# Eight taps of a 31-tap convolution moved from VectorE to ScalarE and GpSimd in a one-core decoder step

## The reference, cut to what matters

```python
hn = rmsnorm(x, g_mix)
z = hn @ w_in                       # 1024 -> 5 x 1024: xa, u_glu (two parts), gate_a, gate_b
v = u_glu[..., :D_CONF] * jax.nn.sigmoid(u_glu[..., D_CONF:])
v_c, new_conf = causal_dwconv(v, conf_buf, w_conf_dw, b_conf_dw)    # 31 taps per channel
y_b = jax.nn.silu(layernorm(v_c, g_conf_ln, b_conf_ln)) @ w_conf_pw + b_conf_pw
m = jax.nn.sigmoid(gate_a) * y_a + jax.nn.sigmoid(gate_b) * y_b
h = x + m @ w_out
y = h + moe(rmsnorm(h, g_ffn), ...)          # top 4 of 32 experts
```

## Time and profile before

| | us |
|---|---|
| median of 3 runs (1339.78 to 1343.15) | 1340.11 |
| span of the profiled execution | 1338.6 |
| TensorE busy (matmuls) | 1295.3, 97% |
| VectorE busy | 508.0, 38% |
| ScalarE busy | 179.5, 13% |
| GpSimd busy | 79.1, 6% |

### The profile page before, as it was taken

One profiled execution on the slowest core, in us unless ns is written; L12 is line 12 of the kernel. 1 busy time (PEld: TensorE's weight loads), 2 busy tenths in 40 slices (PEclk: granted clock), 3 DMA queues, 4 the chain that ended last, 5 costly groups with the idle time before them and its releaser, 6 DMA issues.

```text
span 1338.6 us, 19293 instructions
## 1 busy us (share of the span) xinstructions
PE 1295.3 (97%) x7441; PEld 648.4 (48%) x7442; DVE 508.0 (38%) x981; ACT 179.5 (13%) x325; POOL 79.1 (6%) x107
## 2 busy tenths in 40 slices
PE   6999689999999999999999999999999999999996
PEld 4777467564544444444444444444444444443532
DVE  2899996542232232232323232222222232223232
ACT  3111126220100000101000000000000000010102
POOL 2532220120000000000000000000000000000000
PEclk9999889999999999999999999999999999999999
DMA  9934312468999999999898989898989898989671
GB/s 291 322 127 152 136 63 95 190 248 342 396 414 374 413 374 388 398 361 423 364 417 360 419 358 418 357 422 364 423 362 423 355 422 356 420 357 421 261 316 37
DMA packets 84376, 439.59 MB, mean 328 GB/s; under 512 B 7983, under 2 KB 30639, under 8 KB 35427
## 3 DMA queue, kind: packets, MB, share of 16 engines
q1 hardware_dynamic: 83219, 437.11, 81.4%
q0 software_dynamic: 976, 1.96, 0.5%
q10 hardware_dynamic: 144, 0.00, 0.0%
HBM read 437.46 MB, written 2.43 MB: 329 GB/s over the span
## 4 chain that ended last, share of the span: by engine, by line
PE 82%; DVE 8%; issue 6%; ACT 2%; DVEq 1%; DMA 0%; POOL 0%; SPq 0%; ACTq 0%; POOLq 0%
PE ps L1001 33%; PE ps L1060 16%; PE ps L979 11%; PE ps L1084 7%; PE ps L992 4%; DVE ws L1305 4%; PE ps L788 4%; PE ps L1053 3%; PE ps L910 2%; PE ps L805 1%; DVEq L1304 1%; DVE ws L1277 1%; PE ps L918 1%; PE ps L937 0%; DVE ws L1289 0%
## 5 line engine op out<-in xcount | busy, mean ns | idle before, releaser
L1001 PE MATMUL ps<-ring,ws 128*64 128x512 f32 x2032 | 451.5, 594 | 0.0
L1001 PEld LDWEIGHTS ps<-ring,ws 128*64 128x64 f32 x2032 | 141.5, 137 | 298.9 <-issue 298.9
L1060 PE MATMUL ps<-ring,ws 128*64 128x512 f32 x992 | 218.6, 592 | 0.0
L1476 DVE TENSOR_TENSOR acc<-ps,acc 128x1024 f32<-128x1024 f32 x48 | 58.8, 1224 | 285.9 <-PE ps L1084 285.9
L805 PE MATMUL ps<-ws,ring 128*128 128x288 f32 x640 | 159.7, 413 | 0.7 <-issue 0.7
L1456 DVE TENSOR_SCALAR ws<-ps 64x1024 f32<-64x1024 f32 x32 | 38.9, 1217 | 310.5 <-PE ps L1001 310.5
L979 PE MATMUL ps<-ws 128*128 128x64 bf16 x2304 | 145.3, 227 | 0.0
L979 PEld LDWEIGHTS ps<-ws 128*128 128x128 bf16 x2304 | 141.8, 170 | 2.9 <-issue 0.8
L805 PEld LDWEIGHTS ps<-ws,ring 128*128 128x128 f32 x640 | 123.8, 194 | 35.5 <-issue 0.8
L1060 PEld LDWEIGHTS ps<-ring,ws 128*64 128x64 f32 x992 | 71.3, 138 | 143.4 <-issue 143.2
L1305 DVE SCALAR_TENSOR_TENSOR ws<-ws,par x240 | 113.7, 549 | 0.0
(11 more groups left out here) (187 smaller groups left out, 611.2 us busy)
## 6 DMA issues: line engine op xcount, KB each, us to landing
ring<-in_w_gate SPq DMA_DIRECT2D x127, 1024.0 KB, 7.0
ring<-in_w_up SPq DMA_DIRECT2D x127, 1024.0 KB, 9.2
ring<-in_w_down SPq DMA_DIRECT2D x124, 1024.0 KB, 7.0
ring<-in_w_in SPq DMA_DIRECT2D x20, 1024.0 KB, 11.3
ring<-in_w_conf_pw SPq DMA_DIRECT2D x4, 1024.0 KB, 6.4
ring<-in_w_out SPq DMA_DIRECT2D x4, 1024.0 KB, 6.7
ws<-in_w_down SPq DMA_DIRECT2D x2, 1024.0 KB, 9.5
acc<-in_x_prompt SPq DMA_DIRECT2D x2, 512.0 KB, 4.2
```

Source lines behind the costliest of these rows:

```text
L1001: ins = nc.tensor.matmul(ps[m * CAP:(m + 1) * CAP, bk + h, :], x_e[:, b, 2 * q + t, :], w[:, m, t, h * 512:(h + 1) * 512], start=False, st ...
L1060: ins = nc.tensor.matmul(ps[h * CAP:(h + 1) * CAP, bk, :], hid_t[:, b, k, :], w[:, h * 512:(h + 1) * 512], start=False, stop=(k == NT - 1))
L1476: V.tensor_tensor(acc[:, i, :], ps[:, bk:bk + 2, :].rearrange("p h n -> p (h n)"), acc[:, i, :], ALU.add).then_inc(s_add, 1)
```

## The change

The prompt's taps are split: `KV` = 23 taps (0 to 22) stay with VectorE, eight (23 to 30) go elsewhere. For each tile ScalarE makes eight products of 256 columns, each a copy with a per-channel scale, into two groups of four "lanes". GpSimd folds them: group 0 += group 1 (1024 columns), the first two lanes += the last two (512), then lane 0 + lane 1 (256) into `part`. VectorE adds `part` to its own sum at the end of each pair of tiles.

The lanes use the memory of `gate_a`, `part` that of the first 2048 words after it, where `st_v`, the rows of new state, are put later. So there are new waits: ScalarE's products of a tile wait for the gated unit (`s_v`) and for the fold of the tile before (`s_fold`), its first gate waits for all folds, and its copies of the state rows wait for the whole convolution (`s_conv`, `N_CONV`). ScalarE makes the products of two tiles after the `vb` of the second. GpSimd folds after the gated units of a pair and before the tap products of that pair (for the first pair, after them).

```diff
+LANES = 4
+KV = KC - 2 * LANES
...
+        lanes = ga_w[:, 0:2 * LANES * T_P].rearrange("p (g l t) -> p g l t", g=2, l=LANES)
+        part = ga_w[:, TW:TW + NT * T_P].rearrange("p (c t) -> p c t", c=NT)
...
-        CONV_MID = 2 * (KC // 2) + 4
+        CONV_MID = 2 * (KV // 2) + 4
+        CONV_TILE = KV + 3
         N_STORES = 16 * 14
-        N_CONV, N_XC = NT * (KC + 2), 2 * NT * KA
+        N_CONV, N_XC = NT * CONV_TILE, 2 * NT * KA
...
+                def fold(c):
+
+                    for cc in (c, c + 1):
+                        pool.wait_ge(s_lane, 2 * cc + 2)
+                        pool.tensor_tensor(lanes[:, 0], lanes[:, 0], lanes[:, 1], ALU.add).then_inc(s_fold, 1)
+                        pool.wait_ge(s_fold, 3 * cc + 1)
+                        pool.tensor_tensor(lanes[:, 0, 0:2], lanes[:, 0, 0:2], lanes[:, 0, 2:4], ALU.add).then_inc(s_fold, 1)
+                        pool.wait_ge(s_fold, 3 * cc + 2)
+                        pool.tensor_tensor(part[:, cc, :], lanes[:, 0, 0, :], lanes[:, 0, 1, :], ALU.add).then_inc(s_fold, 1)
...
+                    if c:
+                        fold(c)
                     if c == 0:
                         pool.wait_ge(empt_v, EV("par"))
...
+                    if c == 0:
+                        fold(c)
...
+                    if c % 2:
+                        for cc in (c - 1, c):
+                            act.wait_ge(s_v, 2 * cc + 2)
+                            for g in range(2):
+                                if cc:
+                                    act.wait_ge(s_fold, 3 * cc - (2 if g else 0))
+                                for n in range(LANES):
+                                    j = KV + g * LANES + n
+                                    ins = act.activation(lanes[:, g, n, :], vx[:, cc, j:j + T_P], ACT.Copy,
+                                                         scale=par[:, cc, W_DW + j:W_DW + j + 1])
+                                ins.then_inc(s_lane, 1)
...
+                act.wait_ge(s_fold, 3 * NT)
                 for c in range(4):
                     act.activation(gate_a[:, c, :], empty(f"ga{c}")[:, 0:T], ACT.Sigmoid).then_inc(empt_a, 1)
 
+                act.wait_ge(s_conv, N_CONV)
                 for name, st, b, r in (("vp", st_v, 0, HC), ("vs", st_v, 1, T_S), ("xp", st_x, 0, HA),
...
-                    for j in range(KC):
+                    for j in range(KV):
                         past = 0
-                        if j == KC // 2:
+                        if j == KV // 2:
...
+                    dve.wait_ge(s_fold, c * 3 + 6)
+                    for n in range(2):
+                        dve.wait_ge(s_conv, base + (2 * KV + 3 + n))
+                        V.tensor_tensor(vc[:, c + n, 0:T_P], vc[:, c + n, 0:T_P], part[:, c + n, :], ALU.add).then_inc(s_conv, 1)
```

More of the change, by code:

```diff
@@ L246, in build @@
         s_conv = sem("conf_conv_steps")
+        s_lane = sem("tap_products_in_lanes")
+        s_fold = sem("lanes_folded")
         s_tap = sem("sample_tap_products_ready")
@@ L522, in _ @@
                     else:
-                        pool.wait_ge(s_conv, (c - 2) * (KC + 2) + CONV_MID)
+                        pool.wait_ge(s_conv, (c - 2) * CONV_TILE + CONV_MID)
                     for cc in (c, c + 1):
@@ L553, in _ @@
                     if c == 1 or c % 2 == 0:
-                        pool.wait_ge(s_conv, (c // 2 + 1) * 2 * (KC + 2))
+                        pool.wait_ge(s_conv, (c // 2 + 1) * 2 * CONV_TILE)
                     if c > 1:
@@ L1281, in _ @@
                     dve.wait_ge(s_v, c * 2 + 4)
-                    base = c * (KC + 2)
-                    for j in range(KC):
+                    base = c * CONV_TILE
+                    for j in range(KV):
                         past = 0
-                        if j == KC // 2:
+                        if j == KV // 2:
                             dve.wait_ge(s_tap, c + 2)
@@ L1295, in _ @@
                             past = 4
-                        elif j > KC // 2:
+                        elif j > KV // 2:
                             past = 4
@@ L1303, in _ @@
                             else:
-                                dve.wait_ge(s_conv, base + (2 * (j - 1) + n + 1 + (past if j != KC // 2 else 0)))
+                                dve.wait_ge(s_conv, base + (2 * (j - 1) + n + 1 + (past if j != KV // 2 else 0)))
                                 V.scalar_tensor_tensor(y, x, w, y, ALU.mult, ALU.add).then_inc(s_conv, 1)
+                    dve.wait_ge(s_fold, c * 3 + 6)
+                    for n in range(2):
+                        dve.wait_ge(s_conv, base + (2 * KV + 3 + n))
+                        V.tensor_tensor(vc[:, c + n, 0:T_P], vc[:, c + n, 0:T_P], part[:, c + n, :], ALU.add).then_inc(s_conv, 1)
                 dve.wait_ge(empt_a, EA("xa1"))
```

## The result

| | before | after |
|---|---|---|
| median, us | 1340.38 (4 runs) | 1360.37 (4 runs, 1357.69 to 1361.74) |
| ratio, 95% interval | | 1.0143 [1.0127, 1.0158] |
| span of the profiled execution | 1338.6 | 1358.5 |
| loop of the 31-tap convolution on VectorE | 40.37 to 168.29, 127.9 long | 41.92 to 170.78, 128.9 long |
| subtraction of the mean starts | 173.72 | 193.24 |

The account below looks back on a forecast made before the run. VectorE's convolution was taken to bound the kernel before the mean; folds repay the saved taps and the added wait puts five TensorE jobs behind it: 1338.6 + 19.9 + 1.5 = 1360.0 us, range 1351 to 1368.

Parts of the forecast that it names:

- VectorE alone: 31-tap convolution on VectorE: 64 steps removed save 25.5 us, eight additions cost 3.2, so 22.3 us shorter.
- What the folds take: GpSimd's fold additions beside VectorE's convolution: 14336 columns at 1.87 ns take 26.9 us of VectorE's time, bounds 24.2 and 31.1.
- What leaves the loop: GpSimd's channel-tile sums (L557) move behind the convolution, giving VectorE back 2.7 us.
- Loop: VectorE's 31-tap convolution: 129.8 us long, ending at 170.2 instead of 168.3 (167.5 and 174.4 with the bounds).
- Other engines: GpSimd needs 26 us a pair against VectorE's 32.4 and keeps ahead; TensorE's ga0 may stand 1 to 5 us, covered.
- The added wait: ScalarE's state-row copies wait for the convolution; five TensorE jobs start at 170.8, the mean ends at 193.6: +19.9 us.
- The rest moves along: After the mean's subtraction: gate blocks, w_out and its successors, expert loads included, move by the same 19.9 us.
- The rule of the prediction: Whole kernel: time follows the convolution's end; the change needs an end before 150.3 to gain.
- folds that cost little: Rival: long GpSimd additions let VectorE's steps through, convolution ends at 143.3, time 1333.1, gain 7 us; 7 in 100.
- the cases between: Folds take 7 to 20 us of VectorE's time, kernel time 1340 to 1353; 8 in 100.
- GpSimd as the bound: Rival: at 10 us a fold GpSimd needs 36 us a pair, VectorE waits, time 1372; 10 in 100.
- the hidden wait: Rival: TensorE's five jobs don't stand behind the bank of vp0, the mean waits for GpSimd alone, 1351.1; 3 in 100.

Follow-up runs that it names:

- without folds: The changed kernel with each GpSimd fold addition cut to one column per lane, products and waits kept, folded taps left out of the result: 1333.4 us, ratio 0.9929.
- the same additions beside 31 taps: The kernel before, all taps on VectorE, plus three GpSimd additions per tile (1024, 512, 256 columns) on data nobody else uses: 1371.5 us, ratio 1.0213.
- The wait alone: The kernel before plus one line, ScalarE's state-row copies waiting for the whole convolution: 1357.6 us, ratio 1.0108.
- short folds: The changed kernel with the same sums, every fold addition cut into pieces of 256 columns, seven a tile instead of three: 1356.7 us, ratio 1.0120.
- four taps: The changed kernel with four taps per tile moved instead of eight, folded sums in memory of their own, without the added wait: 1343.7 us, ratio 1.0021.
- eight and ten taps on TensorE: The kernel before with eight or ten taps per tile of the last pair multiplied on ScalarE, summed on TensorE: 1333.9 and 1330.8 us.
- neither folds nor wait: The changed kernel with one-column folds (folded taps left out) and sums in memory of their own, so without the added wait: 1321.3 us, ratio 0.9855.
- sums in memory of their own: The changed kernel, complete, with part in the gate-block weights' memory, loaded after the convolution, so state-row copies don't wait for it: 1345.2 us, ratio 1.0021.
- twelve taps: The kernel before with twelve taps per tile of the last pair multiplied on ScalarE and summed on TensorE: 1334.6 us, ratio 0.9951.

## Why the prediction was right

It said 1360.0 and the time was 1360.4. By its steps:

- **VectorE alone** (64 steps fewer, eight additions more: 22.3 us saved). Before, less the sums' 3.2 us, is 124.7; without folds it is 101.6. That is 23.2 saved. With GpSimd quiet the additions took 0.75 for two.
- **What the folds take** (26.9, within 24.2 and 31.1). 128.9 - 101.6 = 27.3 us, 1.90 ns a column. The row of L557, nearest in operands, gave 1.87 and was close; the same additions beside 31 taps cost 2.02, so the agreement to 0.4 us is better than the method. The Trainium skill has an exclusive lock on the shared port pair, held for a whole instruction (SBUF — State Buffer, section "Who interferes with whom"). The trace agrees in kind: unrelated additions on GpSimd lengthened the loop by 29.0 us, and two steps lost 2.17 us beside a 1024-column addition of 2.44. It doesn't agree with the price that the prediction drew from the rule, whole durations (31.1): part of the standing is GpSimd's, as the additions of 3.38 and 3.94 us show. The prediction's sign for the 1024-column fold, 2.1 to 2.5 us, held for five of the eight; the others took 2.53, 2.72 and 3.38.
- **What leaves the loop** (2.7). The wait alone measured 3.2.
- **Loop** (129.8, to 170.2). 128.9, to 170.8. The forecast was 0.9 too long; but the loop began 1.5 later than before, because TensorE's first 32 w_in instructions took 10.98 us and not 9.76 (and began 0.3 later). In the other runs they took 9.47 to 11.05, whatever the edit, so I take it for no effect of the change. In each microsecond from 21 to 24 us three of these instructions are under way, and not five or six as before, while the granted clock reads 1.00 in both profiles; the cause stays open.
- **Other engines** (GpSimd 26 us a pair, margin 6; `ga0` stands 1 to 5 us). GpSimd's last taps waited 8.4 us for VectorE, and `ga0` stood 4.7. Both as said. A second short stand, 3.2 us before the state rows (they need columns that GpSimd packs until 143.35), I had not named; it was covered too.
- **The added wait** (five jobs at 170.8, 22.1 us long with the clock, then the mean). They started at 171.6 and took 21.1, so the subtraction was at 193.24 for 193.6 forecast. The clock, as the earlier trace rows before and here after:

```profile
155.00:171.00 16.00, 0.00 (x0) 0.00 (x0) 16.00 (x39) 0.10 (x1) 0.00 (x0) 0.50 0.00 0
171.00:173.00 2.00, 1.43 (x3) 1.17 (x4) 2.00 (x9) 2.00 (x5) 0.54 (x1) 0.50 0.00 0
...
175.00:177.00 2.00, 2.00 (x10) 1.56 (x9) 0.28 (x2) 0.00 (x0) 2.00 (x5) 1.00 0.16 27
```

  After 22.8 us idle TensorE was at 1.2 GHz (0.50) when work came, at 0.63 on average from 173 to 175 and at 2.4 GHz (1.00) from 175. The five jobs lost 1.5 us by it (21.07 for 19.57); the forecast had 2.5, with the mean's part.
- **The rest moves along** (19.9). w_out started at 264.00, 19.4 after the 244.59 of before. It ran at the lower clock there, 4.94 us for 3.66, 1.3 more that was not in the forecast; of these 20.7 us some 0.8 were made up later, and the span grew by 19.9.

So the mechanism was right, and the agreement to 0.4 us is in part luck: the late start of the loop (1.5) and the clock at w_out (1.3) were not in the forecast, and the shorter loop (0.9), the cheaper clock (1.0) and the 0.8 at the end go the other way.

The split that the prediction gave only as a sum is now measured, each median against before beside it. Both in place: 20 us slower. With the wait and without folds it is 8 faster, so folds cost 28 us on top of the wait; with folds and without the wait 4 slower, so the wait costs 16 on top of the folds. Both away is 20 faster. Alone, wait and folds on the kernel before cost 16 and 30.

The rule of the prediction, "time = 1340.1 + (end of the convolution - 150.3)" held where the wait was present: 1332.7 for no folds (measured 1333.4), 1356.4 for the wait alone (1357.6), 1356.3 for short folds (1356.7). All three lie 0.4 to 1.2 us over the rule, and so does before beside them (1341.3 and 1341.4 for 1340.1).

The rivals: folds that cost little, and the cases between (7 to 20 us), fell by the 27.3 and 29.0 us; GpSimd as the bound by the 8.4 us that it waited; the hidden wait by the wait alone. Their shares (7, 10 and 3 in 100) can't be judged from one case.

## What to carry to other kernels

VectorE's multiply-adds and GpSimd's additions, both on SBUF, weren't parallel work here (1.9 to 2.0 ns of VectorE per GpSimd column): before moving one to the other, price the GpSimd columns at what a VectorE step loses beside them, from any overlap in the trace. Summing tree-wise on GpSimd took 1792 columns for eight products of 256, almost a column for each column moved, so it gave back all that it took. And when a new buffer borrows the memory of a later one, follow the wait through every in-order queue: here one line on ScalarE held five jobs of TensorE and cost as much as a real piece of work. TensorE had a hole of 15.8 us; given the sums of ten taps in the last pair, it took them without slowing VectorE, and the kernel was 0.7% faster (ratio 0.9929).

## What the runs showed of the hardware that was not expected

TensorE's clock at w_out. In every profile TensorE stands 2.4 to 2.8 us before it, for VectorE's last merge. In some profiled executions the 64 instructions then take 3.66 us (before, four taps, eight and ten taps on TensorE, neither folds nor wait), in the others 4.94 to 5.35. The length of the stand doesn't sort them: in the run with sums in memory of their own it was 2.36 with the fall, in that with neither folds nor wait 2.83 without. The windows of before and of after show the difference in the granted clock:

```profile
244.00:246.00 2.00, 1.41 (x28) 1.08 (x32) 0.38 (x1) 1.05 (x2) 0.24 (x1) 1.00 1.01 426
```

```profile
264.00:266.00 2.00, 2.00 (x20) 1.09 (x24) 0.00 (x0) 0.87 (x2) 0.84 (x2) 0.50 1.00 422
```

So up to 1.7 us of any difference between two profiles can come from here, 0.13% of the time and as much as the half-widths of the intervals. It may not belong to the kernel: there is one profile of each, and the executions of the kernel before alone had, in the runs beside ten and twelve taps, a mean granted clock of 0.980 (1343.15 us) to 0.987 (1339.07 us). What decides it stays open.
